# Router in plain fp32 on turned rows of x, pairwise gather of expert tokens, and a token-major last projection in a four-layer trunk kernel

## What is computed

```python
for i in range(4):
    h = rms_norm(x, norm_mix[i])
    x = x + mixer(h)        # i%3: 0 stick-breaking attention, 1 S5 with GLU, 2 latent attention
    h = rms_norm(x, norm_ffn[i])
    x = x + (swiglu(h) if i % 2 == 0 else moe_swiglu(h))
return rms_norm(x, final_norm)

def moe_swiglu(hf, w_router, b_router, w_gate_up, w_down):   # 8 experts, 1024 -> 2 x 1408 -> 1024
    logits = hf @ w_router + b_router
    top_v, top_i = top_k(logits, 2)
    gates = one_hot(top_i) * softmax(top_v)
    return sum(gates[:, e:e+1] * swiglu(hf, w_gate_up[e], w_down[e]) for e in range(8))
```

## Time and profile before

| | us |
|---|---|
| median of 3 runs | 1813.26 |
| lowest and highest | 1809.82 and 1814.19 |
| the profiled execution | 1812.86 |
| its span in the trace | 1811.3 |
| TensorE (PE) busy | 1730.5 (96%) |
| VectorE (DVE) busy | 1280.3 (71%) |
| ScalarE (ACT) busy | 999.3 (55%) |

### The profile page before, as it was taken

The page is one execution under the profiler, slowest core; times in us unless marked ns, Lnnn a source line. Parts: engine busy times, 40 slices in busy tenths (PEclk is TensorE's granted clock), DMA queues, the critical chain, the costliest instruction groups (busy, mean ns, idle before and its releaser), DMA issues. The chain is left out here.

```text
span 1811.3 us, 26464 instructions
## 1 busy us (share of the span) xinstructions
PE 1730.5 (96%) x10785; PEld 1590.3 (88%) x10785; DVE 1280.3 (71%) x1245; ACT 999.3 (55%) x883; POOL 253.5 (14%) x294
## 2 busy tenths in 40 slices
PE   7989999999899999999899999999988999999997
PEld 7969999789699999999788999998876999999995
DVE  5567898783668888888866455446525888888887
ACT  5364343433467777777544353334464767777774
POOL 5838960000000000000210000000020000000010
PEclk9999999999999999999999999999999999999998
DMA  7526786664369999998833054455503799999984
GB/s 293 207 75 231 250 297 227 239 244 152 125 243 358 351 369 357 362 346 349 348 143 136 35 207 177 140 192 181 191 30 117 290 352 358 359 357 362 363 353 175
DMA packets 53756, 450.12 MB, mean 249 GB/s; under 512 B 6768, under 2 KB 8976, under 8 KB 16928
## 3 DMA queue, kind: packets, MB, share of 16 engines
q1 hardware_dynamic: 48480, 430.40, 62.9%
q0 software_dynamic: 5184, 18.40, 2.7%
HBM read 427.67 MB, written 21.10 MB: 248 GB/s over the span
## 5 line engine op out<-in xcount | busy, mean ns | idle before, releaser
L365 DVE TENSOR_TENSOR wlo<-raw,whi 128x3072 fp32r<-128x3072 f32 (+1 forms) x278 | 855.1, 3079 | 247.8 <-ACT whi L358 247.5
L358 ACT ACTIVATE whi<-raw 128x3072 fp32r<-128x3072 f32 (+1 forms) x278 | 706.3, 2542 | 402.0 <-PE PS L315 383.4
L313 PE MATMUL PS<-wlo,hT_hi 128*128 128x384 f32 (+2 forms) x1936 | 627.8, 324 | 8.5 <-DVE hT_lo L1984 7.4
L315 PE MATMUL PS<-whi,hT_hi 128*128 128x384 f32 (+2 forms) x1936 | 624.4, 323 | 0.0
L314 PE MATMUL PS<-whi,hT_lo 128*128 128x384 f32 (+2 forms) x1936 | 624.3, 322 | 0.0
L313 PEld LDWEIGHTS PS<-wlo,hT_hi 128*128 128x128 f32 x1936 | 367.6, 190 | 14.3 <-DVE hT_lo L1984 7.9
L314 PEld LDWEIGHTS PS<-whi,hT_lo 128*128 128x128 f32 x1936 | 367.6, 190 | 3.2 <-issue 0.2
L315 PEld LDWEIGHTS PS<-whi,hT_hi 128*128 128x128 f32 x1936 | 367.4, 190 | 0.3
L313 PE MATMUL PS<-wlo,mhi 128*128 128x512 f32 x352 | 143.6, 408 | 2.4 <-DVE mlo L1997 2.4
L315 PE MATMUL PS<-whi,mhi 128*128 128x512 f32 x352 | 139.2, 395 | 0.0
L314 PE MATMUL PS<-whi,mlo 128*128 128x512 f32 x352 | 139.1, 395 | 0.0
(11 more groups left out here) (372 smaller groups left out, 2022.8 us busy)
## 6 DMA issues: line engine op xcount, KB each, us to landing
raw<-in_weights SPq DMA_DIRECT2D x203, 1536.0 KB, 7.3
raw<-in_weights SPq DMA_DIRECT2D x73, 1024.0 KB, 7.0
raw<-s_tables SPq DMA_DIRECT2D x8, 1536.0 KB, 7.9
expert_rows<-ysb POOLq DMA_DIRECT2D x14, 512.0 KB, 6.9
s_tables<-g_out SPq DMA_DIRECT2D x8, 640.0 KB, 4.8
t_af<-s_rows_af SPq DMA_DIRECT2D x32, 128.0 KB, 4.0
s_tables<-g_out SPq DMA_DIRECT2D x8, 512.0 KB, 4.7
raw<-in_weights SPq DMA_DIRECT2D x3, 1152.0 KB, 5.7
```

The costliest lines, as they stand in the source:

```text
L313: pe.matmul(o, sh, mlw, start=start, stop=False, skip_group_check=True)
L315: return pe.matmul(o, sh, mh, start=False, stop=stop, skip_group_check=True)
L358: act.activation(whi[p0 % SPL][:, 0:n], raw[p0 % RAW][:, 0:n], ACT.Copy).then_inc(hi_done, 1)
L365: dve.tensor_tensor(wlo[p0 % SPL][:, 0:n], raw[p0 % RAW][:, 0:n], whi[p0 % SPL][:, 0:n].bitcast(F32), ALU.subtract).then_inc(lo_done, 1)
```

## The change

1. **Router.** The norm of n = 3 and n = 7 no longer makes h. TensorE turns the raw x (`turn_x`, partly within the projection ahead), ACT and DVE copy the eight turned blocks to `xT` (plain fp32), and the logits are eight fp32 products of `wr` (router weights times the norm's gain, multiplied by Pool beforehand, padded to 32 columns) with `xT`, each to one of four 32-partition strips of bank 1. One more product with a 0/1 matrix (`C_SEL`) adds the strips and turns them. The factor 1/rms multiplies the logits afterwards. `hh` and `hl` are now x times 1/rms, without the gain.
2. **Squares.** The sum of squares is formed in parts, the first 768 columns ahead of the last add.
3. **Projection ahead of n = 7** (`routed_proj_*`) runs all three pieces for tokens 0 to 127 and then for 128 to 255, and turns six blocks in between. In the S5 stage the last columns' gate is handled by token halves.
4. **Gather.** `gather(e+1)` serves two experts at once and yields turned tokens directly: 32 products of 256 columns, with `hh`/`hl` as the stationary operand, in banks 6, 7, 1, 2. It stands behind u3 of the odd expert and waits for the last `mact` (bank 2). `turn_tokens` and `gt` are gone. ACT and DVE split with the gain as scale (`pair_hi`, `pair_lo`, 8 instructions each).
5. **Splits ahead of expert 0.** DVE writes `wlo` of two pieces behind the first `pick` in n = 3, and of three in n = 7.
6. **Rows of the experts.** `yg` has two tiles in place of four. Pool fetches the first rows, waits for `add_rows(0)`, and then fetches the second. `add_rows(0)` moves to j = 2 of expert 7, `add_rows(1)` stays behind `alo(3)`.
7. Router weights lie in the `gain` tile and are loaded stages earlier; some waits are added for reused memory (`s5_rd`, `s5_parT` ahead of the first `sp` and `pw` write).

```diff
+        def routed_proj_pe(pe, b0, ready):
+            for t in range(TT):
+                for i, (c0, w) in enumerate(DCOLS):
...
+                        if t == 1 and i == len(DCOLS) - 1 and k == KC // 2:
+                            pe.wait_ge(x_most, 2)
+                            turn_x(pe, 7, range(6))
...
         def moe_pe(pe, m, n):
-            pe.wait_ge(m_lo, 3 * m + 1)
+            if n == 3:
+                turn_x(pe, n, (4, 5))
+            for t in range(TT):
+                x_ready(pe, n, t)
+            turn_x(pe, n, (6, 7))
+            pe.wait_ge(m_wg, m + 1)
             for k in range(KC):
...
+                r = slice(32 * (k % 4), 32 * (k % 4) + 32)
+                last = pe.matmul(PS[r, 1, 0:L], wr[:, k, :], xT[:, k, :], start=(k < 4), stop=(k >= 4),
+                                 skip_group_check=True)
...
+            def gather(e, banks):
                 g = NE * m + e
-                pe.wait_ge(ex.pick, g + 1)
+                pe.wait_ge(ex.pick, g + 2)
...
+                for k in range(KC):
+                    o = PS[:, banks[k // 2], (k % 2) * L:(k % 2 + 1) * L]
                     for t in range(TT):
...
+                        mv = mo["pick"][:, t].rearrange("p i s -> p (i s)")
+                        pe.matmul(o, mo["hh"][:, t, k * P:(k + 1) * P], mv, start=(t == 0), stop=False, skip_group_check=True)
+                        last = pe.matmul(o, mo["hl"][:, t, k * P:(k + 1) * P], mv, start=False, stop=(t == TT - 1),
+                                         skip_group_check=True)
...
                 for j in range(1, JE):
-                    if j == JE - 1 and not last_e:
-                        gather(e + 1)
                     pe.wait_ge(ex.silu, JE * g + j)
                     gate_or_up("g", j)
-                    if j == JE - 1 and not last_e:
-                        turn_tokens(e + 1)
                     turn(j - 1)
                     if j >= 2:
                         down(j - 2)
                     gate_or_up("u", j)
+                if par == 1 and not last_e:
+                    pe.wait_ge(ex.mul, JE * g + JE)
+                    gather(e + 1, NEXT_BANKS)
                 down(JE - 2, JE - 1)
...
+            def pair_lo(e, banks):
                 g = NE * m + e
...
+                for q, bank in enumerate(banks):
+                    dve.wait_ge(ex.ghi, 4 * g + 2 * q + 2)
+                    for k in (2 * q, 2 * q + 1):
+                        dve.scalar_tensor_tensor(out=hT_lo[:, k, :], in0=PS[:, bank, (k % 2) * L:(k % 2 + 1) * L],
+                                                 scalar=gain_of(n, k), in1=hT_hi[:, k, :].bitcast(F32),
+                                                 op0=ALU.mult, op1=ALU.subtract).then_inc(ex.glo, 1)
...
+                    if j == JE - 1 and par == 1 and not last_e:
+                        sp_("u", j)
+                        alo(j)
+                        pair_lo(e + 1, NEXT_BANKS)
+                        continue
                     if j == JE - 1:
-                        add_rows(0) if last_e else glo(e + 1, 1 - par)
                         alo(j)
                         if last_e:
                             add_rows(1)
                     sp_("u", j)
...
+                    if j == JE - 2 and last_e:
+                        add_rows(0)
...
             pick(0)
-            for p0 in held_back(n, 2):
+            for p0 in held_back(n, 2 if n == 3 else 3):
                 split_lo(dve, p0)
...
-            for t in range(TT):
-                for j in range(2):
-                    pool.indirect_dma_start(YG[:, 2 * t + j, :], None, y_mem[:, :],
+            for j in range(2):
+                if j == 1:
+                    pool.wait_ge(ex.added, 2 * m + 1)
+                for t in range(TT):
+                    pool.indirect_dma_start(YG[:, t, :], None, y_mem[:, :],
```

More of the change, by code:

```diff
@@ L551, in norm_dve @@
                                          in1=gain[:], op0=ALU.mult, op1=ALU.mult).then_inc(nrm_h, 1)
[L552 to L562, removed]
-                for p0 in held_back(n, 2):
-                    split_lo(dve, p0)
+            for p0 in held_back(n, 2):
+                split_lo(dve, p0)
         def norm_pool(pool, n):
@@ L1467, in s5_pe @@
                     for t in range(TT):
+                        if i == 2 and q == 1 and t == 1:
+                            pe.wait_ge(x_most, 1)
+                            turn_x(pe, 3, range(4))
                         for k in range(KC):
@@ L1869, in expert @@
                     sp_("d", JE - 1)
-            gathered(0)
-            ghi(0, 0)
+            pair_hi(0, FIRST_BANKS)
             expert(0, True, False, 0)
-            with act.Fori(1, NE - 2, 2) as e:
-                expert(e, False, False, 1)
-                expert(e + 1, False, False, 0)
+            expert(1, False, False, 1)
+            with act.Fori(1, NE // 2 - 1) as pair:
+                expert(2 * pair, False, False, 0)
+                expert(2 * pair + 1, False, False, 1)
+            expert(NE - 2, False, False, 0)
             expert(NE - 1, False, True, 1)
@@ new lines, in pick @@
+            def pick(e):
+                if type(e) is int and e == 0:
+                    at_slot = lambda i, a, t: route[:, i, a, t:t + 1]
+                else:
+                    src = route[:, e:e + 2, 0:2, :] if type(e) is int else route[:, bass.ds(e, 2), 0:2, :]
+                    dve.tensor_copy(mo["cur"][:], src).then_inc(ex.cur, 2)
+                    dve.wait_ge(ex.cur, (NE - 2) * m + e)
+                    at_slot = lambda i, a, t: mo["cur"][:, i, a, t:t + 1]
+                for i in range(2):
+                    for t in range(TT):
+                        last = dve.tensor_scalar(mo["pick"][:, t, i, :], IOTA, at_slot(i, 0, t), at_slot(i, 1, t),
+                                                 ALU.is_equal, ALU.mult)
+                last.then_inc(ex.pick, 2)
@@ L2034, in moe_dve @@
             pick(0)
-            for p0 in held_back(n, 2):
+            for p0 in held_back(n, 2 if n == 3 else 3):
                 split_lo(dve, p0)
-            for t in range(TT):
-                i = dve.tensor_tensor(route[:, :, 2, t], oh[:, t, 0, :], oh[:, t, 1, :], ALU.add)
-            link(i)
-            glo(0, 0)
+            pair_lo(0, FIRST_BANKS)
+            weights()
             link(dve.tensor_reduce(mo["cmx"][:], PS[:, 3, 0:NE], AX.X, ALU.max))
@@ L2045, in moe_dve @@
             where()
[L2046 to L2048 removed]
+            expert(1, False, False, 1)
+            with dve.Fori(1, NE // 2 - 1) as pair:
+                expert(2 * pair, False, False, 0)
+                expert(2 * pair + 1, False, False, 1)
+            expert(NE - 2, False, False, 0)
             expert(NE - 1, False, True, 1)
```

435 lines of the change are left out of this document (269 added, 166 removed).

## The result

Over twenty executions each, the changed kernel takes 1815.20 us (1810.15 to 1820.31) and the kernel before 1809.83 (1807.32 to 1814.19). The ratio is 1.0026, 95% interval 1.0018 to 1.0035: 0.26% slower, inside the 0.3% that was counted as no change, where 1800 was forecast.

A forecast was written before the change was run, and what follows sets the result against it. PE, busy 96% of the span, was taken to bound the kernel. From the profiled 1812.86 us, -8.6 - 5.1 - 3.2 + 3.8 - 0.3 = -13.4 gave 1799.5, rounded 1800, range 1791 to 1809.

The forecast's parts named there:

- the starts: From the projection's end to expert 0's first product: 8.6 us less in n = 3, 5.1 less in n = 7.
- the router's products: In the start of n = 3: 16 records take 0.65 us, at most 3.4 if serial.
- Gathers within the loops: In both expert loops: three gathers per stage, each 3.84 us behind a 1.9 us wait, save 1.6 us per stage.
- Rows of the experts: In expert 7: second rows land later and cost 3.8 us in n = 3; n = 7 gains 0.3 us.
- Rival C: At the gathers within the loops: the wait costs 0.6 us instead of 1.9, total 1792 us; chance 0.08.
- Rival D: In expert 7: rows late in both stages, +8 and +4 us, total 1808 us; chance 0.12.
- Rival B: In expert 7 of n = 3: second rows in time, -1.9 us in place of +3.8, total 1794 us; chance 0.15.
- Rival E: At six pair boundaries: slower `pair_hi` and `pair_lo` delay the next expert, 3.2 us each, total 1819 us; chance 0.07.

The follow-up runs named there:

- `wait_late`: Changed kernel with the gather's wait for the last mact moved from ahead of all 32 products to ahead of the last 8: 1792.79 us (0.9891).
- `mact_first`: Changed kernel with DVE, in the odd experts within the loops, multiplying the last mact before the 2048-wide split, not after: 1797.64 us (0.9922).
- `warm_gather_short`: Changed kernel with three unread products of 512 columns ahead of the gather's wait in the six places within the loops: 1806.42 us (0.9967).

## Why the prediction was wrong

**What bounds the kernel, and the starts.** Right. Forecast -8.6 and -5.1, in the traces -9.0 and -5.0, with PE released by `hT_lo` behind DVE's splits. Within the sum one term was small: the router's products took 1.2 us, not 0.65 (L1814, from 473.54 to the copy at 474.78), and smaller errors the other way cancelled it. One thing was left out in n = 3: PE's wait ahead of expert 0 was shorter than before, the half clock fell into the gather (0.57 from 481 to 485) instead of into expert 0, and the first product to the first turn took 12.6 us in place of 15.4, another -2.8. That is luck of the execution: of ten profiles with this start the half clock fell into the first gather in six, into expert 0 in three, and at neither in one. In n = 7 it cancelled, as forecast.

**Gathers within the loops: the step that failed.** Forecast -1.6 per stage. The prediction saw the wait, its cause and nearly its length (1.9, measured 2.1 to 2.3), and worked out the products' time at full clock rightly (3.84, measured 3.83 in `wait_late`). What it left out is what an idle PE does to the next products: half clock for some 3 of the gather's 5.4 us, 1.6 more. It knew of this at the starts, where it priced 3 us; for the gathers it put the term at nothing, without a reason. Measured are 23.0 us per stage (three waits of 2.1 to 2.3 and three times 5.4) against 7 x 2.71 = 19.0, +4.0, 11 us worse than forecast over both stages. `wait_late`, `mact_first` and `warm_gather_short` show it from three sides. Rival C, by which the wait costs 0.6, didn't come true; `mact_first`, which makes the wait that short, took 1797.6. That `wait_late` took rival C's 1792 is chance: there PE waited 11.39 us for `ylo` in n = 3, 8.1 more than before, where rival C had 3.8.

The Trainium skill, "TensorE: Matmul & The Clock Gate", section "HAM oscillation — how this bites in real kernels", describes a loop in which each tile's wait for DMA throttles PE again, so that the price is paid in every pass and not once. The traces agree in kind: paid at 15 of 18 gathers over three profiles. It should have stood among the rivals.

**Rows of the experts.** The mechanism was right, the term too small. Forecast +3.8 in n = 3, measured 9.87 - 3.25 = +6.6; -0.3 in n = 7, measured 1.66 - 0.08 = +1.6. The second transfer landed 10.6 us after its own issue, within, but that issue came 4.3 us after the first, and DVE wanted the rows at 890.4, only 3.3 us after it. The forecast had the landing 13.5 us behind the first issue and the rows wanted 8 to 9 behind it; measured are 14.9 (897.78 - 882.92) and 7.5. So its 5 us of lateness were 7.4. Rival D, rows late in both stages, put both too high (+8 and +4) but was right that n = 7 would pay. Rival B, by which they would be in time, is refuted. The Trainium skill's fit ("DMA: Bandwidth & Descriptors", "Anatomy of one DMA — SWDGE (gpsimd) path", an estimate of 3.2 us for 512 KB) doesn't hold for these indirect transfers: median 10.5 us here. Even the last two of n = 7, issued after the last weight piece had landed (1780.8), took 7.6 and 5.7.

**Rival E**, the slower one, had the right places (each pair, six times) and the wrong mechanism: in no profile does PE wait 0.3 us or more at g0, u0 or g1 of the next expert, and in n = 7 eight `pair_lo` took 3.2 us.

**The sum by traces:** -9.0, -5.0 and -2.8 at the starts; +8.0 gathers; +8.2 rows; +0.9 in the rest of the two stages; the remaining -1.2 lie outside the two stages: +1.7 ahead of n = 3, -2.2 between them, -0.7 behind. There the half clock fell at other places (365 after and not before; 976 and 1013 before, granted 0.57 and 0.58, and 1.00 there after). That is -0.9.

**The medians** are 6 us further apart than the traces. The base of the sum was one profiled execution, which lies 3.0 above the median of twenty; the three executions known then (1809.82 to 1814.19) didn't tell. A range for the median should have carried this spread on both sides. The executions of the changed kernel spread more (10 us against 7). A clock that falls at some gathers and not at others would do that in part, but it isn't the whole: the slowest (1820.31) had a mean granted clock of 0.979 and the fastest (1810.15) 0.980, 2 us of full clock apart where the times are 10 apart. No profile of one of the slowest was taken: the rest stays open.

## What to carry to other kernels

Price each new wait of TensorE twice, once for its length and once for what the clock does to the products behind it; here a wait of 2.3 us, repeated in a loop, cost 3.9. Before merging several small waits into one, look whether the wait is needed by all products behind it or by the last ones alone. When a buffer is saved by fetching in two steps, count from the issue of the last transfer to the instruction that wants it.

## What the runs showed of the hardware

- The granted clock fell to 0.50 after waits of 2.1 to 2.8 us at 15 of 18 gathers, and at none of six after 0.5 to 0.7 us; a wait of 2.3 us filled with unread products didn't bring it about. The same wait is followed by it in one execution and not in another.
- A plain fp32 product of 512 columns took 0.86 us (two records, 0.43 apart, at a granted clock of 1.00), one on rounded fp32 operands of 512 columns 0.23.
- The stretch at half clock can fall into a part where it costs nothing: at the start of n = 3 it lay in the first gather, beside DVE's splits, in six of ten profiles, and in expert 0 in three. The waits ahead of it are 0.5 to 1.0 us each there, among unread products, so a short wait alone doesn't keep the clock up everywhere.
- An indirect transfer of 128 rows took 8.6 to 17.2 us from issue to landing beside weight loads in the first profiles of the two kernels, and 5.7 and 7.6 without them (n = 7 of the changed kernel).
